# The value projection of an encoder layer by tokens: 128 weight columns moving in place of 384 tokens

## The chip, the cores and the metric

The kernel runs on one core of one Trainium2 chip. The metric is the device time of one execution in microseconds (us), the median of several runs. Before the change it is 1993.51 us, the median of 3 runs (1993.31 to 1993.57).

## What is computed

The kernel does one inference step of a hybrid encoder layer, for 1024 prompt tokens and 128 sample tokens that share the weights. The part that matters here is the projection in front of the forgetting attention, and what becomes of its third piece, the values:

```python
def _in_proj(x, g, w_in, b_f):
    z = _rmsnorm(x, g) @ w_in
    q, k, v, f, u, qm, gates = jnp.split(z, _split_points(), axis=-1)
...
    s = jnp.einsum('bqhd,bkhd->bhqk', q.astype(jnp.float32), k.astype(jnp.float32)) * scale
    s = s + jnp.transpose(cq, (0, 2, 1))[:, :, :, None] - jnp.transpose(ck, (0, 2, 1))[:, None, :]
    s = jnp.where(kpos[None, :] <= qpos[:, None], s, -jnp.inf)
    p = jax.nn.softmax(s, axis=-1)
    o = jnp.einsum('bhqk,bkhd->bqhd', p, v.astype(jnp.float32))
```

The model width is 1024, the values are 512 wide (8 heads of 64). The keys and the values are also outputs, tokens by channels.

## The kernel before

**Tiles.** The normalised activations lie in SBUF with channels on the 128 partitions: `act`, 8 tiles of 128 channels by 1152 tokens (1024 and 128). Each fp32 matrix is kept as two fp32r parts, high and low, and a product is three matmuls (`COMBOS`): high by high, high by low, low by high. A column block of weights is 8 tiles of 128 by 128 (`w_raw`, split by ScalarE and VectorE into `w_hi` and `w_lo`, two sets in turn).

**The plan.** `plan` is a list of steps, written in an order that all engines follow. A step of kind "q", "k", "v", "gate" and so on is one column block of weights by all 1152 tokens. It fills three PSUM banks, one for each 384 tokens. TensorE (`product`, L1230) takes the 128 by 128 weight tile as the stationary operand and 384 tokens of `act` as the moving one, 8 channel tiles by 3 combinations by 3 blocks, so 72 matmuls. The result has channels on the partitions and tokens along them. Each step is cut in `halves`, and work of another kind (attention, sampling, pooling) is put in between them by the table `beside`: before part x of a step, each engine does what is listed for (kind, i, j, x). A bank is used again three blocks later, when it has been emptied (`emptied`).

**A pair of heads.** For each of four pairs of heads (`for p in range(BT)`), the plan has q, k, v, then "kturn" and "vturn", then gate and branch products in which the pair's attention runs (`fox`, 19 pieces). The values leave their bank by a VectorE copy into `vf` (L2078), channels by tokens. In "kturn" and "vturn" TensorE turns keys (`kf`, L1262) and values (`vf`, L1257), three blocks of three 128 by 128 transposes each, in three banks. The turned keys are copied into one of five buffers `tok` by ScalarE (L1598), the turned values by VectorE (L2084). Out of `tok`, the sync engine stores them in DRAM (L766 and L768), and for the values ScalarE makes the high part of `fox_v` (L1635) and VectorE the low part (`values_lo`, L2044). The attention's first scores (L984) stand right behind, in part 0 of the first gate step; VectorE reads them (L1829), ScalarE takes the exponent (L1390). The value product of the attention (L997) takes `fox_v` as one operand.

**What orders them.** `tok_use` numbers the uses of the `tok` buffers, `tok_full` counts them in that order, and `tok_stored` tells when one has been stored. Before, the keys' three come first, then the values' three. `load_negc` loads the attention's bias for pair 0 in part 3 of the first "v" step.

Of the kernel before, what the change touches and what calls it, by code (L numbers as in the profile page):

```python
# [12 lines left out]
P = 128  # L13
# [19 lines left out]
def encoder_program(nc, x_prompt, x_sample, mem_prompt, cache_fox_k, cache_fox_v, cache_fox_logf, cache_pool,  # L33
# [95 lines left out]
    for p in range(BT):  # L129
        add("q", p, src=win[:, :, p * P:(p + 1) * P], hi=3)  # L130
        add("k", p, src=win[:, :, FW + p * P:FW + (p + 1) * P], hi=3)
        add("v", p, src=win[:, :, 2 * FW + p * P:2 * FW + (p + 1) * P])
        add("kturn", p, halves=3)
        add("vturn", p, halves=3, hi=3)
        merge_tile(0, 2 * p)
        merge_tile(0, 2 * p + 1)
    for h in range(MH):
# [65 lines left out]
    with ExitStack() as ctx:  # L203
# [84 lines left out]
        fk = tensor("fox_k", [P, 2, SEQ], R2_AT + 16384, F32R)  # L288
        fv = tensor("fox_v", [P, QT, 4, FD], R2_AT + 24576, F32R)
        kf = tensor("fox_kf", [P, T], R_AT + 8192)  # L290
        vf = tensor("fox_vf", [P, T], R2_AT + 32768)
        fot = tensor("fox_ot", [P, 2 * P], R3_AT + 13824)


# [105 lines left out]


        def tok_use(kind, i, j):
            return {"memturn": i, "kturn": 2 * MH + 6 * i + j, "vturn": 2 * MH + 6 * i + 3 + j,
                    "qm": 2 * MH + 6 * BT + 3 * i + j}[kind]

        def tok_buf(n):
# [12 lines left out]
        def tok_free(eng, kind, i, j, n):  # L419
            k = tok_buf(n)  # L420
            if tok_sent[n]:
                eng.wait_ge(tok_stored[k], tok_sent[n])
            if kind == "kturn" and j == 0 and i:
                for m in range(2):
                    eng.wait_ge(prod_stored[m], 16 * 3 * i)

# [119 lines left out]
        def _(sp):  # L546
# [180 lines left out]
            for s in plan[FIRST:]:  # L727
                for x in range(s.halves):
                    if x == 0 and s.c >= 2:
                        load_weights(sp, s.c + 2)  # L730
                    if s.kind == "qm" and s.i == 0 and x == 4:
                        refill(0)
                    if s.kind == "gate" and s.i == 2 and s.j == 0 and x == 0:
                        refill(1)
                    if s.kind == "q" and s.i and x == 0:
                        load_negc(s.i)
                    if s.kind == "v" and s.i == 0 and x == 3:
                        load_negc(0)
                    if s.kind == "out" and x == 0 and s.i + 1 < KT:
                        load_xtok(s.i + 1)  # L740
                    if s.kind == "br" and s.i == 2 and s.j == KT - 2 and x == 0:
                        load_xtok(0)
                    if s.kind == "gate" and s.i and x >= 3 and (s.i, s.j) != (2, 1):
                        load_prev(s.i, s.j, x - 3)
                    if s.kind == "br" and (s.i, s.j) == (2, 0):
                        load_prev(2, 1, x)
                    for what in beside.get((s.kind, s.i, s.j, x), ()):
                        beside_sp(*what)
                    if s.kind == "memturn" and s.i % 2 == 0:
                        emptied(sp, at["memkv", s.i, 0].b)  # L750
                        sp.dma_start(mem_kt[:, s.i // 2, :], kst[0][:]).then_inc(kst_stored, 16)
                    if s.kind in ("memturn", "kturn", "vturn") or s.kind == "qm" and x % 2:
                        j = x // 2 if s.kind == "qm" else x
                        n = tok_use(s.kind, s.i, j)
                        buf, stored = (tok_q if s.kind == "qm" else tok)[tok_buf(n)], tok_stored[tok_buf(n)]
                        sp.wait_ge(tok_full, n + 1)
                        cs = slice(s.i * P, (s.i + 1) * P)
                        if s.kind == "memturn":
                            cs = slice(s.i // 2 * P, (s.i // 2 + 1) * P)
                            sp.dma_start((mv_out if s.i % 2 else mk_out)[:, :, cs], buf[:, 0:MT, :]).then_inc(stored, 16)  # L760
                        elif s.kind == "qm":
                            sp.dma_start(mem_q[:, s.i, cols(j)], buf[:].rearrange("p t c -> p (t c)")).then_inc(stored, 16)
                        else:
                            big, rest = (kp_out, ks_out) if s.kind == "kturn" else (vp_out, vs_out)
                            tiles = min(3, QT - 3 * j)
                            sp.dma_start(big[:, 3 * j:3 * j + tiles, cs], buf[:, 0:tiles, :]).then_inc(stored, 16)  # L766
                            if j == 2:
                                sp.dma_start(rest[:, cs], buf[:, 2, :]).then_inc(stored, 16)  # L768
                    if s.kind == "br" and s.i < 2:
                        i = 3 * s.j + x  # L770
                        if s.i == 0:
                            emptied(sp, s.b + x)
                        else:
                            sp.wait_ge(mg["added"], i + 1)
                        src = (prod1 if s.i else prod0)[i % 2]
                        sp.dma_start(merged[s.i, s.j, :, cols(x)], src[:]).then_inc(prod_stored[i % 2], 16)
                if s.kind == "k" and s.i == 0:
                    sp.wait_ge(po["tail"], BT)
                    sp.dma_start(new_pool_p.rearrange("l a j c -> (l a j) c"),
                                 p_tail[P - HIST:P, 0, :]).then_inc(po["stored"], 16)  # L780
                    for i in range(NB):
                        sp.dma_start(new_pool_s.rearrange("l b j c -> (l b) j c")[i],
                                     p_tail[(i + 1) * NQ - HIST:(i + 1) * NQ, 1, :]).then_inc(po["stored"], 16)
                if s.kind == "last" and s.i == 0 and s.j == 0:
                    finished(sp, s.b - 1)
                    sp.dma_start(g_y[:], g_final.partition_broadcast(P)).then_inc(g_in["fin"], 16)
# [110 lines left out]
        def _(pe):  # L897
# [348 lines left out]
            def turned(s, x):  # L1246
                b = s.b + x
                emptied(pe, b - 3)
                dst = bank(b)
                if s.kind == "memturn":  # L1250
                    emptied(pe, at["memkv", s.i, 0].b)
                    for t in range(MT):
                        last = nc.tensor.transpose(dst[:, t * P:(t + 1) * P], kst[s.i % 2][:, t * P:(t + 1) * P], ident[:])
                elif s.kind == "vturn":
                    emptied(pe, at["v", s.i, 0].b + x)
                    for t in range(3):
                        last = nc.tensor.transpose(dst[:, t * P:(t + 1) * P], vf[:, (3 * x + t) * P:(3 * x + t + 1) * P],  # L1257
                                                   ident[:])
                else:
                    emptied(pe, at["k", s.i, 0].b + x)  # L1260
                    for t in range(3):
                        last = nc.tensor.transpose(dst[:, t * P:(t + 1) * P], kf[:, (3 * x + t) * P:(3 * x + t + 1) * P],  # L1262
                                                   ident[:])
                last.then_inc(blk_over, 1)

            for s in plan[FIRST:]:
                for x in range(s.halves):
# [2 lines left out]
                    j = x * s.blocks // s.halves  # L1270
                    if s.kind == "memkv":
                        product(s, x, ME, width=NMEM)
                    elif s.kind in ("memturn", "kturn", "vturn"):
                        turned(s, x)
                    elif s.kind == "br":
                        if s.j == 0 and s.i == 0:
                            pe.wait_ge(po["mix_lo"], 3 * BT)
# [27 lines left out]
        def _(act):  # L1305
# [251 lines left out]
            def leave(s, j):  # L1557
# [20 lines left out]
                if s.kind == "br":  # L1578
# [2 lines left out]
                        act.wait_ge(mg["added"], 3 * KT + i + 1)  # L1581
                        nc.scalar.activation(M[0][:, s.j, cols(j)], prod1[i % 2][:], ACT.Copy, scale=0.5).then_inc(mg["hi"], 1)
                    return
                if s.kind in ("v", "down", "last"):
                    return
                finished(act, b)
                if s.kind == "memkv":
# [5 lines left out]
                elif s.kind in ("memturn", "kturn"):  # L1593
                    n = tok_use(s.kind, s.i, j)
                    tok_free(act, s.kind, s.i, j, n)
                    w = MT if s.kind == "memturn" else 3
                    act.wait_ge(tok_full, n)
                    nc.scalar.activation(tok[tok_buf(n)][:, 0:w, :], src[:, 0:w * P].rearrange("p (t c) -> p t c", c=P),  # L1598
# [17 lines left out]
                elif s.kind in ("q", "k"):  # L1616
# [11 lines left out]
                            act.wait_ge(po["tail"], BT)  # L1628
                        last = nc.scalar.activation(rest[0][:, s.i, :], src[:, LAST:TB], ACT.Copy, scale=scale)
                    last.then_inc(ev_hi, 1)  # L1630
                elif s.kind == "vturn":
                    w = min(3, QT - 3 * j)
                    n = tok_use(s.kind, s.i, j)
                    act.wait_ge(tok_full, n + 1)
# [45 lines left out]
        def _(dve):  # L1680
# [369 lines left out]
            def leave(s, j):  # L2050
# [20 lines left out]
                elif s.kind == "v":  # L2071
                    finished(dve, b)
                    if j == 0 and s.i == 0:
                        dve.wait_ge(kst_stored, 16 * MH)
                        finished(dve, at["memturn", 2 * MH - 1, 0].b)
                    elif j == 0:
                        dve.wait_ge(at_s["t_over"], 16 * s.i)
                    nc.vector.tensor_copy(vf[:, cols(j)], src).then_inc(free, 1)  # L2078
                elif s.kind == "vturn":
                    n = tok_use(s.kind, s.i, j)  # L2080
                    finished(dve, b)
                    tok_free(dve, s.kind, s.i, j, n)
                    dve.wait_ge(tok_full, n)
                    nc.vector.tensor_copy(tok[tok_buf(n)][:].rearrange("p t c -> p (t c)"), src).then_inc(tok_full, 1)  # L2084
# [101 lines left out]
```

## Time and profile before

| | |
|---|---|
| median of 3 runs | 1993.51 us (1993.31 to 1993.57) |
| the profiled execution | 1993.0 us, its span from first to last instruction 1991.3 us |
| TensorE matmul busy, share of the span | 98% |
| TensorE weight load busy | 96% |
| VectorE, ScalarE, GpSimd busy | 50%, 32%, 10% |
| TensorE's share of the chain that ended last | 86% |
| mean granted clock of TensorE | 0.997 |

All rows come from one profiled execution. Times in the trace are from the span's start. PE is TensorE's matmul, PEld its weight load, which has rows of its own; DVE is VectorE, ACT ScalarE, SPq the sync engine's issues. The end of a matmul in the trace is modelled, and its start is put down when it was handed to the array; where the array still loads its weights the row becomes longer by that.

### The profile page before, as it was taken

How to read it: one execution, taken by the hardware profiler on the slowest of the kernel's cores; microseconds unless marked ns; L12 is line 12 of the kernel's file. 1: busy time of each engine (PE TensorE's matmuls, PEld its weight loads, DVE VectorE, ACT ScalarE, POOL GpSimd, SP SyncE). 2: the span in 40 equal slices, each digit the busy share in tenths (PEclk: the TensorE clock that was granted, in tenths of full speed). 3: DMA queues.
4: the chain of work that ended last, by engine and by line, in shares of the span. 5: the costliest groups of instructions: out<-in, count | busy, mean ns of one | idle time of the engine just before them, and what ended most of it. 6: DMA issues, size and time to landing. Idle time of an engine off the chain costs nothing.

```text
span 1991.3 us, 28760 instructions
## 1 busy us (share of the span) xinstructions
PE 1950.5 (98%) x11667; PEld 1918.1 (96%) x11667; DVE 987.4 (50%) x1886; ACT 630.6 (32%) x1198; POOL 195.3 (10%) x280
## 2 busy tenths in 40 slices
PE   7999999999999999999999999999999999999998
PEld 7999999999989999999999999999999999999998
DVE  6675545454556465554333455444444444444434
ACT  6444434353545444442223332111111111111112
POOL 0003324251511122000000000000000000000000
PEclk9999999999999999999999999999999999999999
DMA  6451312213166533443233211111101020202202
GB/s 183 117 130 49 90 46 65 79 38 106 34 232 193 188 112 103 147 156 106 83 93 96 71 43 38 33 53 32 53 29 58 27 59 27 59 27 59 70 22 96
DMA packets 208664, 164.24 MB, mean 82 GB/s; under 512 B 15374, under 2 KB 186382, under 8 KB 208533
## 3 DMA queue, kind: packets, MB, share of 16 engines
q1 hardware_dynamic: 208533, 162.41, 26.9%
q8 instruction: 93, 1.52, 0.3%
q14 instruction: 38, 0.31, 0.1%
HBM read 132.86 MB, written 29.51 MB: 82 GB/s over the span
## 4 chain that ended last, share of the span: by engine, by line
PE 86%; DVE 5%; issue 3%; ACT 3%; POOL 2%; DMA 1%; SPq 0%; DVEq 0%; POOLq 0%; ACTq 0%
PE ps L1240 72%; PE ps L1224 3%; PE ps L1076 2%; PE ps L1064 2%; PE ps L997 1%; PE ps L1007 1%; PE ps L1031 1%; POOL fox_p L861 1%; PE ps L912 1%; PE ps L1146 1%; PE ps L984 1%; DVE xs L1693 0%; ACT w_hi L443 0%; ACT fox_pt_hi L1397 0%; PE ps L1133 0%
## 5 line engine op out<-in xcount | busy, mean ns | idle before, releaser
L1240 PE MATMUL ps<-act_hi,w_hi 128*128 128x384 f32 x1800 | 612.5, 340 | 2.0 <-DVE fox_q_lo L2063 0.9
L1240 PE MATMUL ps<-act_hi,w_lo 128*128 128x384 f32 x1800 | 603.6, 335 | 0.0
L1240 PE MATMUL ps<-act_lo,w_hi 128*128 128x384 f32 x1800 | 603.2, 335 | 0.0
L1240 PEld LDWEIGHTS ps<-act_hi,w_hi 128*128 128x128 f32 x1800 | 338.8, 188 | 3.7 <-issue 3.0
L1240 PEld LDWEIGHTS ps<-act_lo,w_hi 128*128 128x128 f32 x1800 | 339.0, 188 | 0.7
L1240 PEld LDWEIGHTS ps<-act_hi,w_lo 128*128 128x128 f32 x1800 | 338.6, 188 | 0.0
L443 ACT ACTIVATE w_hi<-w_raw 128x512 fp32r<-128x512 f32 (+1 forms) x172 | 147.0, 855 | 303.6 <-PE ps L1240 300.8
L461 DVE TENSOR_TENSOR w_lo<-w_raw,w_hi 128x512 fp32r<-128x512 f32 (+1 forms) x172 | 168.1, 977 | 132.5 <-ACT w_hi L443 132.5
L1240 PE MATMUL ps<-ff_hi,w_hi 128*128 128x384 f32 x672 | 227.1, 338 | 0.0
L1240 PE MATMUL ps<-ff_lo,w_hi 128*128 128x384 f32 x672 | 227.1, 338 | 0.0
L1240 PE MATMUL ps<-ff_hi,w_lo 128*128 128x384 f32 x672 | 227.1, 338 | 0.0
L2145 DVE TENSOR_TENSOR h<-ps,h 128x384 f32<-128x384 f32 x192 | 107.0, 557 | 222.2 <-PE ps L1240 198.7
L1576 ACT ACTIVATE ff_hi<-ff_r 128x384 fp32r<-128x384 f32 x96 | 50.4, 525 | 325.7 <-DVE ff_r L2134 325.7
L2134 DVE SCALAR_TENSOR_TENSOR ff_r<-ps,rstd 128x384 f32<-128x384 f32 x96 | 53.5, 557 | 185.1 <-PE ps L1240 185.1
L1240 PEld LDWEIGHTS ps<-ff_hi,w_lo 128*128 128x128 f32 x672 | 126.3, 188 | 0.0
L1240 PEld LDWEIGHTS ps<-ff_hi,w_hi 128*128 128x128 f32 x672 | 126.3, 188 | 0.0
L1240 PEld LDWEIGHTS ps<-ff_lo,w_hi 128*128 128x128 f32 x672 | 126.3, 188 | 0.0
L861 POOL TENSOR_SCALAR fox_p<-fox_p,small 128x128 f32<-128x128 f32 (+7 forms) x64 | 110.5, 1726 | 94.0 <-DVE small L1808 92.2
L1240 PE MATMUL ps<-branch_hi,w_hi 128*128 128x384 f32 x288 | 99.8, 347 | 0.0
L1240 PE MATMUL ps<-branch_hi,w_lo 128*128 128x384 f32 x288 | 96.7, 336 | 0.0
L1240 PE MATMUL ps<-branch_lo,w_hi 128*128 128x384 f32 x288 | 96.4, 335 | 0.0
L1813 DVE TENSOR_TENSOR fox_pt_lo<-ps,fox_pt_hi 128x128 fp32r<-128x128 f32 (+7 forms) x64 | 48.4, 757 | 71.6 <-ACT fox_pt_hi L1397 71.6
(308 smaller groups left out, 2821.4 us busy)
## 6 DMA issues: line engine op xcount, KB each, us to landing
w_raw<-in_w_in_dram SPq DMA_DIRECT2D x44, 512.0 KB, 4.3
w_raw<-in_w_up_dram SPq DMA_DIRECT2D x32, 512.0 KB, 4.1
w_raw<-in_w_down_dram SPq DMA_DIRECT2D x56, 256.0 KB, 2.7
merged<-prod SPq DMA_DIRECT2D x48, 192.0 KB, 1.9
prev<-merged SPq DMA_DIRECT2D x48, 192.0 KB, 4.3
foxs_kraw<-in_cache_fox_k_dram SPq DMA_DIRECT2D x8, 1024.0 KB, 5.6
foxs_vraw<-in_cache_fox_v_dram SPq DMA_DIRECT2D x8, 1024.0 KB, 5.8
out_dram<-fin_y SPq DMA_DIRECT2D x9, 512.0 KB, 2.6
```

The costliest lines, as they stand in the source:

```text
L443: nc.scalar.activation(W[c % 2][0][:, 0:kt, :], w_raw[c % 2][:, 0:kt, :], ACT.Copy).then_inc(w_hi, 1)
L461: nc.vector.tensor_tensor(W[c % 2][1][:, 0:kt, :], w_raw[c % 2][:, 0:kt, :], W[c % 2][0][:, 0:kt, :].bitcast(F32), ALU.subtract).then_inc( ...
L861: nc.gpsimd.tensor_scalar(p, p, col(RC, u), None, ALU.mult).then_inc(at_s["p_ready"], 1)
L912: last = nc.tensor.matmul(bank(s.b)[:, 0:TB], W[k][a][:, t, :], A[z][:, t, cols(s.j)], start=(t == 0 and n == 0), stop=(t == KT - 1 and n ...
L1064: last = nc.tensor.matmul(ps[:, 2 + z, 0:w], stat, b["kt"][y][:, j, z * w:(z + 1) * w], start=first, stop=end)
L1076: last = nc.tensor.matmul(ps[:, 4, :], b["pt"][x][:, t, :], b["v"][y][:, t, :], start=(n == 0 and t == 0), stop=end)
L1224: last = nc.tensor.matmul(bank(s.b)[:, 0:TB], LW[a][:, t, s.j * P:(s.j + 1) * P], AC[(NCH - 1) % 2][z][:, t, cols(s.i)], start=(t == 0 and ...
L1240: last = nc.tensor.matmul(bank(b)[:, 0:width], W[k][a][:, t, :], moving[z][:, t, j * width:(j + 1) * width], start=(t == 0 and n == 0), st ...
L1576: nc.scalar.activation(AC[s.i % 2][0][:, s.j, cols(j)], ff_r[i % 2][:], ACT.Square).then_inc(ff["hi"], 1)
L1813: nc.vector.tensor_tensor(dst[1][:, 0:blocks, cs], turned_tiles()[:, 0:blocks, :], dst[0][:, 0:blocks, cs].bitcast(F32), ALU.subtract).the ...
L2134: nc.vector.scalar_tensor_tensor(out=ff_r[i % 2][:], in0=src, scalar=0.0, in1=rstd[:, cols(j)], op0=ALU.max, op1=ALU.mult).then_inc(free, 1)
L2145: nc.vector.tensor_tensor(h, src, h, ALU.add).then_inc(free, 1)
```

## The change

The "v" step's matmuls exchange their operands: 128 tokens of `act` are the stationary operand, and the 128 columns of a weight tile move. The product then has tokens on the partitions and needs no turning. "vturn" is gone; the "v" step has 9 parts, one for each 128 tokens, and three of them fill a bank. VectorE copies a bank of values straight into `tok`, and the rest of the way (store, high part, low part) is as before. The values' `tok` uses are numbered ahead of the keys'.

```diff
-        add("v", p, src=win[:, :, 2 * FW + p * P:2 * FW + (p + 1) * P])
+        add("v", p, src=win[:, :, 2 * FW + p * P:2 * FW + (p + 1) * P], hi=3, halves=9)
         add("kturn", p, halves=3)
-        add("vturn", p, halves=3, hi=3)
...
-            return {"memturn": i, "kturn": 2 * MH + 6 * i + j, "vturn": 2 * MH + 6 * i + 3 + j,
+            return {"memturn": i, "v": 2 * MH + 6 * i + j, "kturn": 2 * MH + 6 * i + 3 + j,
...
-            if kind == "kturn" and j == 0 and i:
+            if kind == "v" and j == 0 and i:
...
-                    if s.kind in ("memturn", "kturn", "vturn") or s.kind == "qm" and x % 2:
-                        j = x // 2 if s.kind == "qm" else x
+                    if s.kind in ("memturn", "kturn") or s.kind == "qm" and x % 2 or s.kind == "v" and x % 3 == 2:
+                        j = x // 2 if s.kind == "qm" else x // 3 if s.kind == "v" else x
...
-                elif s.kind == "vturn":
-                    emptied(pe, at["v", s.i, 0].b + x)
-                    for t in range(3):
-                        last = nc.tensor.transpose(dst[:, t * P:(t + 1) * P], vf[:, (3 * x + t) * P:(3 * x + t + 1) * P],
-                                                   ident[:])
...
+            def values_product(s, x):
+                j, t = divmod(x, 3)
+                if x == 0:
+                    pe.wait_ge(w_lo, s.c + 1)
+                if t == 0:
+                    emptied(pe, s.b + j - 3)
+                for y in range(KT):
+                    for n, (a, z) in enumerate(COMBOS):
+                        last = nc.tensor.matmul(bank(s.b + j)[:, t * P:(t + 1) * P], A[z][:, y, x * P:(x + 1) * P],
+                                                W[s.c % 2][a][:, y, :], start=(y == 0 and n == 0),
+                                                stop=(y == KT - 1 and n == 2))
+                if t == 2:
+                    last.then_inc(blk_over, 1)
...
+                    if s.kind == "kturn" and j == 2:
+                        act.wait_ge(at_s["v_lo"], 3 * s.i + 1)
...
-                elif s.kind == "vturn":
+                elif s.kind == "v":
                     w = min(3, QT - 3 * j)
                     n = tok_use(s.kind, s.i, j)
                     act.wait_ge(tok_full, n + 1)
...
-                    elif j == 0:
-                        dve.wait_ge(at_s["t_over"], 16 * s.i)
-                    nc.vector.tensor_copy(vf[:, cols(j)], src).then_inc(free, 1)
-                elif s.kind == "vturn":
                     n = tok_use(s.kind, s.i, j)
-                    finished(dve, b)
                     tok_free(dve, s.kind, s.i, j, n)
```

## Rows read from the trace of the kernel before

**Rows 1.** The page: busy time by engine, and the chain by engine.

```profile
PE 1950.5 (98%) x11667; PEld 1918.1 (96%) x11667; DVE 987.4 (50%) x1886; ACT 630.6 (32%) x1198; POOL 195.3 (10%) x280
...
PE 86%; DVE 5%; issue 3%; ACT 3%; POOL 2%; DMA 1%; SPq 0%; DVEq 0%; POOLq 0%; ACTq 0%
```

**Rows 2.** The chain in order of time, at the end of a v product.

```profile
159.09 2.08 PE ps L1240 x12
```

**Rows 3.** The tile fox_vf: min/median/max ns, first and last start.

```profile
L1257 PE MATMUL ps<-ident,fox_vf x36: 272/273/329, 167.4 to 489.2; 128*128 128x128 f32 x36
L2078 DVE COPY fox_vf<-ps x12: 557/558/558, 156.0 to 486.6; 128x384 f32<-128x384 f32 x12
```

**Rows 4.** Timeline, matmuls from 181.2 us: start, duration, instruction.

```profile
181.26 0.22 PE L984 MATMUL ps<-fox_k,fox_q_hi 128*128 128x128 f32 x1
181.32 0.27 PE L984 MATMUL ps<-fox_k,fox_q_lo 128*128 128x128 f32 x1
...
181.72 0.22 PE L997 MATMUL ps<-fox_pt_hi,fox_v 128*128 128x128 f32 x1
181.78 0.28 PE L997 MATMUL ps<-fox_pt_lo,fox_v 128*128 128x128 f32 x1
```

**Rows 5.** Timeline, weight loads of the same stretch.

```profile
181.27 0.19 PEld L984 LDWEIGHTS ps<-fox_k,fox_q_lo 128*128 128x128 f32 x1
181.37 0.19 PEld L997 LDWEIGHTS ps<-fox_pt_hi,fox_v 128*128 128x128 f32 x1
181.49 0.19 PEld L997 LDWEIGHTS ps<-fox_pt_lo,fox_v 128*128 128x128 f32 x1
181.61 0.19 PEld L997 LDWEIGHTS ps<-fox_pt_hi,fox_v 128*128 128x128 f32 x1
181.72 0.19 PEld L997 LDWEIGHTS ps<-fox_pt_lo,fox_v 128*128 128x128 f32 x1
```

**Rows 6.** Timeline, TensorE between the v product and the gate product.

```profile
166.05 0.34 PE L1240 MATMUL ps<-act_hi,w_lo 128*128 128x384 f32 x1
166.23 1.36 PE L1262 MATMUL ps<-ident,fox_kf 128*128 128x128 f32 x9
167.43 1.83 PE L1257 MATMUL ps<-ident,fox_vf 128*128 128x128 f32 x9
...
169.51 0.41 PE L1240 MATMUL ps<-act_hi,w_hi 128*128 128x384 f32 x1
```

**Rows 7.** Timeline, ScalarE and VectorE in and behind that gap.

```profile
166.43 0.56 DVE L2078 COPY fox_vf<-ps 128x384 f32<-128x384 f32 x1 [0.85 <-PE ps L1240]
166.76 0.49 ACT L1598 ACTIVATE tok<-ps 128x384 f32<-128x384 f32 x1 [1.83 <-PE ps L1262]
167.44 0.49 ACT L1598 ACTIVATE tok<-ps 128x384 f32<-128x384 f32 x1 [0.19 <-ACT tok L1598]
...
171.37 0.42 ACT L1635 ACTIVATE fox_v<-tok 128x256 fp32r<-128x256 f32 x1 [0.65 <-DVE tok L2084]
171.42 0.89 DVE L2044 TENSOR_TENSOR fox_v<-tok,fox_v 128x384 fp32r<-128x384 f32 x2
171.80 1.28 ACT L1390 ACT_TABLE_LOAD   x1
```

**Rows 8.** Timeline, the first scores of the attention behind the gap.

```profile
172.24 0.28 DVE L1829 CUSTOM_DVE_ANT_0 fox_p<-ps,fox_negc 128x128 f32<-128x128 f32 x1
172.59 0.39 PE L984 MATMUL ps<-fox_k,fox_q_hi 128*128 128x256 f32 x1 [0.74 <-DVE small L1829]
172.67 0.29 POOL L851 COPY fox_negc<-negc_kept 128x128 f32<-128x128 f32 x1 [23.97 <-DVE small L1829]
...
175.32 0.44 PE L984 MATMUL ps<-fox_k,fox_q_hi 128*128 128x384 f32 x1
```

**Rows 9.** Stretches: length, PE, PEld, DVE, ACT, POOL busy (count), PEclk, DMA.

```profile
166.20:169.50 3.30, 2.99 (x22) 2.13 (x20) 1.12 (x2) 1.57 (x4) 0.00 (x0) 1.00 0.33 97
...
560.80:564.00 3.20, 3.20 (x14) 3.20 (x13) 2.92 (x7) 1.09 (x2) 0.00 (x0) 0.55 1.05 391
```

**Rows 10.** Timeline, matmuls inside the stretch of the lower clock.

```profile
562.16 0.53 PE L1240 MATMUL ps<-act_lo,w_hi 128*128 128x384 f32 x1
562.48 0.53 PE L1240 MATMUL ps<-act_hi,w_lo 128*128 128x384 f32 x1
```

More of the change, by code:

```diff
@@ L290, in encoder_program @@
         kf = tensor("fox_kf", [P, T], R_AT + 8192)
-        vf = tensor("fox_vf", [P, T], R2_AT + 32768)
         fot = tensor("fox_ot", [P, 2 * P], R3_AT + 13824)
@@ L1272, in _ @@
                         product(s, x, ME, width=NMEM)
-                    elif s.kind in ("memturn", "kturn", "vturn"):
+                    elif s.kind in ("memturn", "kturn"):
                         turned(s, x)
+                    elif s.kind == "v":
+                        values_product(s, x)
                     elif s.kind == "br":
@@ L1583, in leave @@
                     return
-                if s.kind in ("v", "down", "last"):
+                if s.kind in ("down", "last"):
                     return
@@ L1630, in leave @@
                     last.then_inc(ev_hi, 1)
-                elif s.kind == "vturn":
+                elif s.kind == "v":
                     w = min(3, QT - 3 * j)
```

## The prediction

> **What bounds the kernel now.** I read the page first. TensorE is the bound: matmuls lie over 98% of the span, weight loads over 96%, and 86% of the chain that ended last is TensorE's; VectorE has 50% and ScalarE 32% [rows 1]. So whatever TensorE gains or loses in the "v" steps reaches the end nearly in full, and work taken from the other engines counts only where TensorE waits for it. Next I read the chain in order of time at the end of a "v" step, for the price of the old product: twelve matmuls with 384 moving columns take 2.08 us, 0.1733 us each [rows 2]. Then I went to the tile that goes, for what its turning costs [rows 3], and to the timeline for the nearest thing to the new product, fp32r matmuls with only 128 moving columns; they exist in the attention's scores and in its value product [rows 4, 5]. Last I read the gap between the value product and the gate product, and the stalls behind it [rows 6, 7, 8].
>
> **The old product.** Four pairs, 72 matmuls each: 72 x 0.1733 = 12.48 us a pair.
>
> **The new product.** 9 token tiles x 8 channel tiles x 3 combinations = 216 matmuls a pair, each with its own load of 128 weight columns. It moves the same number of columns in all, 72 x 384 = 216 x 128. It needs three times as many weight loads. The question is what spaces such matmuls: their columns or their loads. The start times of the matmuls say 0.06 us (181.26 to 181.32, 181.72 to 181.78) [rows 4]. But that start is not the array's. Behind a load that is not yet done the row begins early and grows: of the last two matmuls the first has 0.22 us and the second 0.28. Their ends, 181.94 and 182.06, are 0.12 apart. The loads tell the same: five of them follow each other at 0.10, 0.12, 0.12 and 0.11 us, 0.45 over four, so 0.1125 each [rows 5], although two of the four matmuls between them move 128 columns alone. In the old product a load has 0.1733 us to hide in and costs nothing; over 128 columns it sticks out. I take 0.1125 us: 216 x 0.1125 = 24.3 us. Extra: 24.3 - 12.48 = 11.8 us a pair, 47.3 us for four. Bounds: the shortest and the longest spacing of those loads, 0.10 and 0.12, give 21.6 and 25.9 us, so 36.5 and 53.8 us for four pairs. This step decides the forecast. The granted clock stays at 1.00 through the gap with its transposes [rows 9], so I let the new stream run at the full clock too.
>
> The Trainium skill has a rule that speaks against this change ("TensorE: Matmul & The Clock Gate", section "LDWEIGHTS (loading the stationary operand)"): a weight load takes its column count over 1.2, in ns, so 107 ns for 128 columns. By that the product would take 216 x 0.107 = 23.1 us, an estimate from the page, 1.2 us under mine; the rows of the loads agree with it within 0.01 us.
>
> **What is taken out.** The 9 transposes of values a pair (36 in all) [rows 3]. Nine of keys and nine of values lie between the last value matmul's slot, which ends at 166.05 + 0.17 = 166.22, and the gate product at 169.51 [rows 6]. Of its first row's 0.41 us some 0.07 is the wait for its load (the usual row has 0.34), so the gap is 3.36 us. The transposes within a block follow each other at 0.11 us (a block of nine takes 1.36 with its stop and its tail), so 9 x 0.11 = 1.0 us is work; the rest are stops for the copies.
>
> The new gap, with zero where the value product ends: VectorE's copy of the last value bank starts 0.21 us later (166.43) and takes 0.56, so 0.77. ScalarE's copy into `fox_v`, about 0.1 later, takes 0.42: 1.3. Then comes its copy of the first keys' bank, 0.49: 1.8; the bank is free for the gate product about 0.15 later: 1.95 us [rows 7]. TensorE meanwhile turns the keys (third block behind the bank that is empty at 0.8, done by 1.2) and does the first scores, so it waits some 0.5 us. Gap 1.95 in place of 3.36: 1.4 us saved.
>
> **The stalls behind it.** Part 1 of the gate step begins with the second scores, which wait until VectorE has read the first. VectorE is held up by the turned values, low parts to 172.31, so it reads at 172.24 and TensorE starts at 172.59, with about 1.0 us lost: the gate's 12 matmuls of part 0, at 2.08 us from 169.58, would have ended at 171.66 [rows 7, 8]. After the change values 0 and 1 are copied and split under the value product; only the third remains. VectorE is free at about 1.8 us and TensorE asks at 4.0, so the 1.0 us goes. In part 2 there is another stall: 172.94, when the gate goes on behind the second scores, plus 2.08 is 175.02, and the third scores start at 175.32, some 0.3 to 0.4 late [rows 8]. What is late is the chain of ScalarE: table load, exponent, weight split, then VectorE's part. It starts 5.6 us behind the product now (171.80 - 166.22) and 1.3 + 3 x 0.68 = 3.3 us behind it then (the three copies of keys stand 0.68 apart), 2.3 earlier; TensorE also comes 2.4 us earlier. So this stall stays, perhaps 0.1 longer. Sum: 1.4 + 1.0 - 0.1 = 2.3 us a pair, 9.2 for four. Bounds: the transposes alone, 9 x 0.11 x 4 = 4.0, and all stalls gone, 4 x (1.4 + 1.0 + 0.4) = 11.2.
>
> **What costs nothing.** The 12 VectorE copies of 0.56 us [rows 3] lie under TensorE's work; so do the new copies of blocks 0 and 1, with some 8 us of product (24.3 / 3) behind each, which also covers ScalarE's and VectorE's parts of 0.5 and 0.6 us. The splits of the gate's weights, at the start of "v", get more cover than before. On the sync engine's queue the stores of values now stand ahead of `load_negc(0)`, of pair 0 alone, which waits for the first block, some 8 us and a copy into the step. GpSimd was done with its masks 23.97 us before 172.67, at 148.7 [rows 8], and they are needed at the first scores, which come 12 us later than before, so there are some 15 us left for a load and a few masks of 0.29 us. The waits on `tok_stored` meet stores that were issued 8 us or more ahead; the wait of ScalarE in "kturn" for the first low part is long over. The wait for all stores ahead of the gate's first evacuation comes 4 us behind the last issue, as before.
>
> **Sum.** 1993.0 us (the profiled execution, 1991.3 in the span) + 47.3 - 9.2 = 2031.1 us; the median of the runs is 0.5 above that execution, so about 2031.5.
>
> **The rivals.** (a) The loads are hidden after all and the stream runs at the 0.06 us of the start times [rows 4]: 216 x 0.06 = 13.0, +0.5 a pair, +1.9 - 9.2 = -7.3, so 1986 us, faster. Against it stand the ends and the loads' own spacing. It is the case on the other side; it decides from (12.48 + 2.3) / 216 = 0.068 us a matmul downwards. (b) Half of the load is hidden in a long stream, the mean of 0.06 and 0.1125: 0.086 us, 18.6 us a pair, +24.6 - 9.2 = +15.4, so 2009 us. For it: no stretch of before has more than two such matmuls in a row. The Trainium skill states for a stream with a load at each matmul and 128 columns about 81 ns (same page, "Back-to-back issue gap"), by which the time would be 2005 us, an estimate; no row here shows that spacing. (c) Load and stream come one after the other, 0.1125 + 0.06 = 0.1725: 37.3 us a pair, +99.1 - 9.2 = +90, so 2083 us. Against it: in the old product a load would then never be hidden, yet it fits in 0.1733 with 384 columns [rows 2]. (d) The granted clock falls in the new stream. After the wait at 560 it stood at 0.55, the lower level of 1.2 GHz for most of the stretch, and matmuls came 0.32 us apart in place of 0.17 [rows 9, 10], 1.85 times. If the loads slow down likewise: 24.3 x 0.85 x 4 = 83 more, so 2114 us. Against it: it fell only behind a long wait, and there is none in the stream. (e) The load has its price, and the gap gives back only the transposes: 2037 us, inside the range.
>
> **Chances.** My forecast with (e) and the bounds of the load: 0.82. (a) 0.05, (b) 0.05, (c) 0.04, (d) 0.02, anything else 0.02. A difference of 0.2% (4 us) is about what can be told from none. Faster 0.05, same 0.01, slower 0.94. The range: low 1993.5 + 36.5 - 9.2 = 2020.8, high 1993.5 + 53.8 - 4.0 = 2043.3; together 0.82, as wanted, so 2021 to 2043.
>
> **What the profile after will show.** Right: weight loads with `act` stationary and w moving about 0.11 us apart, some 24 us for each v product, matmul rows over 0.2 us in spite of a spacing half as long; TensorE without stops inside a "v" step; a gap of about 2 us up to the gate; no stall at part 1 of the gate and a short one at part 2. Wrong: loads 0.06 to 0.09 apart, a granted clock under 1 inside "v", a wait for a bank at a block's start, or GpSimd late at the first scores of pair 0.

## The result

The changed kernel takes 2031.05 us (median of 4 runs, 2029.74 to 2032.25); the kernel before, measured beside it, 1993.41 (1991.94 to 1993.57). The ratio is 1.0192, with a 95% interval of 1.018 to 1.0204: slower by 37.6 us. The forecast was 2031.5, with 2021 to 2043 as its range. The profiled execution has a span of 2029.1 us, 37.8 more than before.

The page of the changed kernel, its counterpart to [rows 1]:

```profile
PE 1989.2 (98%) x12207; PEld 1959.8 (97%) x12207; DVE 982.6 (48%) x1874; ACT 630.9 (31%) x1198; POOL 196.1 (10%) x280
...
PE 87%; DVE 4%; issue 4%; ACT 2%; POOL 1%; DMA 1%; SPq 0%; ACTq 0%; DVEq 0%; POOLq 0%
```

There are 540 matmuls more: 4 x (216 - 72) = 576, less 36 transposes. In the rows that follow L1268 is the new product, L1238 the ordinary one. The bound is the same engine, and its time has grown.

The chain in order of time in the v step of the second pair, which answers to [rows 2], and the stretch of that step, with the granted clock behind the busy times:

```profile
269.89 23.56 PE ps L1268 x211
```

```profile
269.20:293.20 24.00, 24.00 (x218) 24.00 (x216) 4.50 (x8) 3.03 (x6) 0.00 (x0) 1.00 0.06 17
```

23.56 / 211 = 0.1117 us a matmul, at a clock of 1.00 and without a stop: 216 x 0.1117 = 24.1 us, against 12.48. The weight loads at the end of the first pair's step, which answer to [rows 5], stand 0.11 apart as well:

```profile
176.55 0.19 PEld L1268 LDWEIGHTS ps<-w_lo,act_hi 128*128 128x128 f32 x1
176.67 0.19 PEld L1268 LDWEIGHTS ps<-w_hi,act_hi 128*128 128x128 f32 x1
176.78 0.19 PEld L1268 LDWEIGHTS ps<-w_hi,act_lo 128*128 128x128 f32 x1
176.89 0.19 PEld L1268 LDWEIGHTS ps<-w_lo,act_hi 128*128 128x128 f32 x1
```

TensorE's timeline from the last value matmul on (L1255 the keys' transposes, L982 the scores), answering to [rows 6, 8]:

```profile
176.95 0.28 PE L1268 MATMUL ps<-w_lo,act_hi 128*128 128x128 f32 x1
177.06 1.42 PE L1255 MATMUL ps<-ident,fox_kf 128*128 128x128 f32 x9
178.24 0.31 PE L982 MATMUL ps<-fox_k,fox_q_hi 128*128 128x128 f32 x1
...
178.91 0.41 PE L1238 MATMUL ps<-act_hi,w_hi 128*128 128x384 f32 x1 [0.25 <-ACTq L1613]
...
181.08 0.28 PE L982 MATMUL ps<-fox_k,fox_q_hi 128*128 128x256 f32 x1
...
183.76 0.44 PE L982 MATMUL ps<-fox_k,fox_q_hi 128*128 128x384 f32 x1 [0.19 <-DVE small L1841]
```

The gap goes from 177.06 to 178.98 (178.91 and 0.07 of the long row), 1.92 us in place of 3.36. What ends it is ScalarE's copy of the first keys' bank (L1613 is its release of the bank). The second scores come 181.08 - 178.98 = 2.10 us into the gate step, which is the step's own pace: the stall of 1.0 us is gone. The third come at 183.76; the gate goes on at 181.32, and twelve matmuls from there end at 183.40, so a stall of 0.4 us remains. This second stall is in the first pair only: in the other three, before and after, the third scores follow the gate's matmuls at once. The ScalarE and VectorE rows behind the product, counterparts to [rows 7]:

```profile
177.92 0.42 ACT L1647 ACTIVATE fox_v<-tok 128x256 fp32r<-128x256 f32 x1 [7.52 <-PE ps L1255]
178.24 0.48 ACT L1610 ACTIVATE tok<-ps 128x384 f32<-128x384 f32 x1
178.91 0.49 ACT L1610 ACTIVATE tok<-ps 128x384 f32<-128x384 f32 x1 [0.19 <-ACT tok L1610]
```

```profile
177.26 0.56 DVE L2091 COPY tok<-ps 128x384 f32<-128x384 f32 x1 [6.78 <-PE ps L1268]
177.97 0.89 DVE L2056 TENSOR_TENSOR fox_v<-tok,fox_v 128x384 fp32r<-128x384 f32 x2
```

Before their last piece VectorE was idle for 6.78 us and ScalarE for 7.52: the first two blocks lie wholly under the product.

### The profile page after: what moved, and what is told of

Same layout as the page of the kernel before. It is cut to its first block, busy times and chain, and to the rows that moved or that the text cites. A ratio compares the mean times of both kernels' runs of the same rounds, so it can differ in the third digit from the quotient of the medians.

```text
span 2029.1 us, 29817 instructions
## 1 busy us (share of the span) xinstructions
PE 1989.2 (98%) x12207; PEld 1959.8 (97%) x12207; DVE 982.6 (48%) x1874; ACT 630.9 (31%) x1198; POOL 196.1 (10%) x280
## 4 chain that ended last, share of the span: by engine, by line
PE 87%; DVE 4%; issue 4%; ACT 2%; POOL 1%; DMA 1%; SPq 0%; ACTq 0%; DVEq 0%; POOLq 0%
PE ps L1238 68%; PE ps L1268 5%; PE ps L1222 2%; PE ps L1074 2%; PE ps L1062 2%; PE ps L995 1%; PE ps L910 1%; PE ps L1005 1%; PE ps L1029 1%; POOL fox_p L859 1%; PE ps L1144 1%; PE ps L982 1%; ACT fox_pt_hi L1407 0%; DVE prod L2110 0%; ACT w_hi L441 0%
## 5 line engine op out<-in xcount | busy, mean ns | idle before, releaser
L1238 PE MATMUL ps<-act_hi,w_hi 128*128 128x384 f32 x1704 | 579.7, 340 | 2.3 <-ACTq L1613 1.0
L1238 PE MATMUL ps<-act_hi,w_lo 128*128 128x384 f32 x1704 | 570.7, 335 | 0.0
L1238 PE MATMUL ps<-act_lo,w_hi 128*128 128x384 f32 x1704 | 570.3, 335 | 0.0
L1238 PEld LDWEIGHTS ps<-act_hi,w_hi 128*128 128x128 f32 x1704 | 320.5, 188 | 4.1 <-issue 3.3
L1238 PEld LDWEIGHTS ps<-act_lo,w_hi 128*128 128x128 f32 x1704 | 320.6, 188 | 0.7
L1238 PEld LDWEIGHTS ps<-act_hi,w_lo 128*128 128x128 f32 x1704 | 320.1, 188 | 0.0
L1238 PE MATMUL ps<-ff_hi,w_hi 128*128 128x384 f32 x672 | 227.0, 338 | 0.0
L1238 PE MATMUL ps<-ff_lo,w_hi 128*128 128x384 f32 x672 | 227.0, 338 | 0.0
L1238 PE MATMUL ps<-ff_hi,w_lo 128*128 128x384 f32 x672 | 227.0, 338 | 0.0
L1238 PEld LDWEIGHTS ps<-ff_hi,w_lo 128*128 128x128 f32 x672 | 126.2, 188 | 0.0
L1238 PEld LDWEIGHTS ps<-ff_hi,w_hi 128*128 128x128 f32 x672 | 126.2, 188 | 0.0
L1238 PEld LDWEIGHTS ps<-ff_lo,w_hi 128*128 128x128 f32 x672 | 126.2, 188 | 0.0
L1238 PE MATMUL ps<-branch_hi,w_hi 128*128 128x384 f32 x288 | 99.7, 346 | 0.0
L1238 PE MATMUL ps<-branch_hi,w_lo 128*128 128x384 f32 x288 | 96.7, 336 | 0.0
L1238 PE MATMUL ps<-branch_lo,w_hi 128*128 128x384 f32 x288 | 96.4, 335 | 0.0
```

The source lines that it names most:

```text
L1238: last = nc.tensor.matmul(bank(b)[:, 0:width], W[k][a][:, t, :], moving[z][:, t, j * width:(j + 1) * width], start=(t == 0 and n == 0), st ...
```

## The experiments

All are measured against the kernel before, in runs on the same chip (1991.5 to 1992.6 us there).

**The turning alone (`turn_gone`).** In the changed kernel the product is the old one again, in its usual parts; the main line of the edit:

```diff
-                        values_product(s, x)
+                        product(s, x, A)
```

> The turning taken out alone: the value product stays as it was (72 matmuls of 384 moving columns a pair), its banks go straight into tok, so the value outputs and the attention's values hold channels by tokens; nothing else is left out. Theory (the gap closes and the stall goes): the changed kernel's trace has a gap of 1.92 us in place of 3.36 and no stall at part 1 of the gate step (1.0 us), so 4 x 2.44 = 9.8 us less than before: 1983.6 us. Rival (only the transposes' own work comes back, 36 x 0.11 = 4.0 us): 1989.4 us.

Measured: 1983.03 us against 1992.28, ratio 0.9954 (0.9942 to 0.9967), 9.3 us less. Its timeline behind the product has the changed kernel's gap, from 166.05 to 167.96, and second scores at 170.05, without a stall:

```profile
165.88 0.34 PE L1238 MATMUL ps<-act_hi,w_lo 128*128 128x384 f32 x1
166.06 1.42 PE L1255 MATMUL ps<-ident,fox_kf 128*128 128x128 f32 x9
...
167.89 0.41 PE L1238 MATMUL ps<-act_hi,w_hi 128*128 128x384 f32 x1 [0.25 <-ACTq L1613]
```

The first theory holds. Of the 9.3 us only some 4.0 are the transposes' own time (36 x 0.11, an estimate from their spacing); the rest were stops. With the keys' turning and all copies out of `tok` left as they are, this is what turning the values for nothing would give back.

**The product alone (`product_only`).** In the kernel before, "v" runs `values_product` in 9 parts, and "vturn" and all else stays.

> The product by tokens alone: 216 matmuls a pair with 128 moving columns, and the values are turned all the same, so they reach the attention and the outputs turned the wrong way. Theory (each matmul costs 0.111 us, nothing hides it): 216 x 0.111 = 24.0 in place of 12.48 us a pair, 46.1 us in all: 2039.5 us. Rival (the longer step also gives or takes waits elsewhere, in the sampling stage for one, where the changed kernel lost a further 1 to 2 us): off from that by over 1.5 us.

Measured: 2041.02 us (2038.96 to 2044.25) against 1992.28, ratio 1.0247 (1.0233 to 1.0261). That is 48.7 more, with a spread of 5 us between its runs; 46.1 was expected, and the interval of the ratio (46.4 to 52.0 us) lies just above it. The rival asked for over 1.5 us of difference, and against the kernel before beside it there are 2.6, so it holds. Where the difference arises the trace tells. When the sampling stage begins (its first transpose of cached keys, 606.23 us against 560.07) the kernel is 46.2 us behind, the theory's number, and only at the first matmul with `ff_hi`, the feed-forward's (1317.39 against 1270.12), is it 47.3. The price of the product is thus as forecast, and the rest is picked up in other stages; why there is not shown. The sum of the two halves is -9.25 + 48.74 = 39.5 us, against 37.6 for the whole. The halves add up within the spread of the runs, and whether the 2 us between them are more than that is not settled.

**The values turned first (`values_first`).** The kernel before with two steps exchanged, and the numbers of `tok_use` with them:

```diff
-        add("kturn", p, halves=3)
         add("vturn", p, halves=3, hi=3)
+        add("kturn", p, halves=3)
```

> The kernel before with the values turned ahead of the keys, nothing left out. Theory (the stall of 1.0 us at part 1 of the gate step is VectorE's being held up by the turned values): it goes, and the gap grows by some 0.3 us a pair because ScalarE's first copy of keys now waits for three VectorE copies: 4 x 0.7 = 2.8 us less, 1990.6 us. Rival (VectorE's order does not matter, the stall only moves into the gap): 1993.4 us.

Measured: 1992.02 us against 1992.28, ratio 0.9999 (0.999 to 1.0007). The rival holds: no gain. TensorE's timeline in the gap, here from 166.25:

```profile
166.25 1.42 PE L1257 MATMUL ps<-ident,fox_vf 128*128 128x128 f32 x9
167.59 0.55 PE L1262 MATMUL ps<-ident,fox_kf 128*128 128x128 f32 x3
168.38 0.55 PE L1262 MATMUL ps<-ident,fox_kf 128*128 128x128 f32 x3 [0.25 <-DVEq L2088]
169.56 0.55 PE L1262 MATMUL ps<-ident,fox_kf 128*128 128x128 f32 x3 [0.62 <-DVEq L2088]
...
170.52 0.41 PE L1240 MATMUL ps<-act_hi,w_hi 128*128 128x384 f32 x1 [0.25 <-ACTq L1603]
...
172.68 0.28 PE L984 MATMUL ps<-fox_k,fox_q_hi 128*128 128x256 f32 x1
```

The second scores are in time (172.68 - 170.59 = 2.09), but the gap is 4.34 us in place of 3.36. The last block of keys now waits for a bank that VectorE empties last, and ScalarE copies its first keys only then. So the stall at part 1 did come of VectorE's being late, as read from [rows 7, 8], but order alone only moves the loss into the gap.

**High and low weights side by side (`wide_moving`).** The changed kernel with one matmul of 256 moving columns for two of 128:

```diff
+                            last = nc.tensor.matmul(bank(s.b + x)[:, 0:2 * P], A[0][:, y, x * P:(x + 1) * P],
+                                                    W2[s.c % 2][:, :, y, :], start=(y == 0), stop=(y == KT - 1))
```

> The changed kernel with high and low weights side by side as 256 moving columns: the high activations are loaded once for both, 144 loads a pair in place of 216, same columns; VectorE adds the two halves of a bank. Nothing is left out. Theory (a matmul costs its weight load, 0.111 us, where its columns take less): 72 x (0.120 + 0.111) = 16.6 in place of 24.0 us a pair, 29.5 us less than the changed kernel: 2001.5 us. Rival (128 moving fp32r columns cost 0.111 us by themselves, whatever the loads): 256 columns cost 0.222 and nothing changes: 2031 us.

Measured: 1999.19 us (1998.29 to 2000.59) against 1992.28, ratio 1.0034 (1.0021 to 1.0047), so some 31 us less than the changed kernel, and still 6.9 us more than before. Two loads, one for 256 columns and one for 128, take 0.23 us together:

```profile
270.14 0.19 PEld L1273 LDWEIGHTS ps<-w_both,act_hi 128*128 128x128 f32 x1
270.25 0.19 PEld L1270 LDWEIGHTS ps<-w_both,act_lo 128*128 128x128 f32 x1
270.37 0.19 PEld L1273 LDWEIGHTS ps<-w_both,act_hi 128*128 128x128 f32 x1
```

The same columns with a third fewer loads cost 16.6 us a pair (72 x 0.23) in place of 24.1, so the columns are not the cost. This run has a third fewer matmuls too, and so it can't tell the price of a load from a fixed price of a matmul; `narrow_standing`, below, does.

**Fewer moving columns, or fewer standing ones (`narrow_moving`, `narrow_standing`, `narrow_96`).** In the changed kernel the matmuls with a low part are made smaller, but for the last of each tile (135 of 216 a pair), once in the weights that move (64, and later 96), once in the tokens that stand (64):

```diff
+                        m = P if n == 0 or n == 2 and y == KT - 1 else P // 2
+                        last = nc.tensor.matmul(bank(s.b + j)[:, t * P:t * P + m], A[z][:, y, x * P:(x + 1) * P],
+                                                W[s.c % 2][a][:, y, 0:m], start=(y == 0 and n == 0),
```

> The changed kernel with only 64 weight columns moving in 135 of the 216 matmuls a pair (those with a low part, but for each tile's last), so the low parts are left out for half of the value columns. The loads stay at 128 columns. Theory (the load sets the spacing): no change, 0.111 us each, 2031 us. Rival (the moving columns set it): these take half, 0.056 us, 135 x 0.055 x 4 = 30 us less: 2001 us.

> The changed kernel with only 64 tokens standing in the same 135 matmuls a pair, so the low parts are left out for half of the tokens; all 128 weight columns move. Theory (the load sets the spacing): a load of 64 columns takes half, and the stream of 128 columns (0.06 us) sets it then: 135 x 0.05 x 4 = 27 us less, 2004 us. Rival (the moving columns set it): no change, 2031 us.

Measured: `narrow_standing` 2004.2 us (3 runs, 2003.19 to 2004.38) against 1991.54, ratio 1.0062 (1.0039 to 1.0084), on the theory's 2004. That is 12.7 us more than before, so 25 us less than the changed kernel's 37.6. Its loads of 64 columns stand 0.06 apart, those of 128 0.11, at a clock of 1.00, though there are as many loads, matmuls and moving columns as in the changed kernel. So it is the standing columns, and not the number of matmuls, that are paid for:

```profile
168.53 0.19 PEld L1269 LDWEIGHTS ps<-w_hi,act_hi 128*128 128x128 f32 x1
168.64 0.14 PEld L1269 LDWEIGHTS ps<-w_hi,act_lo 128*64 128x64 f32 x1
168.70 0.13 PEld L1269 LDWEIGHTS ps<-w_lo,act_hi 128*64 128x64 f32 x1
168.76 0.19 PEld L1269 LDWEIGHTS ps<-w_hi,act_hi 128*128 128x128 f32 x1
```

`narrow_moving` 2094.49 us (2 runs, 2094.39 and 2094.58), ratio 1.0516 (1.0485 to 1.0546): half the columns in most of the matmuls, and 63 us slower than the changed kernel. Neither theory nor rival had that. The stretches (length, busy times, and behind them the granted clock), and loads from before and after the fall:

```profile
165.00:170.00 5.00, 5.00 (x45) 5.00 (x45) 1.23 (x3) 0.69 (x2) 1.47 (x5) 1.00 0.11 43
170.00:175.00 5.00, 5.00 (x34) 5.00 (x33) 0.50 (x1) 0.41 (x1) 0.00 (x0) 0.70 0.12 39
175.00:180.00 5.00, 5.00 (x25) 5.00 (x25) 0.00 (x0) 0.00 (x0) 0.00 (x0) 0.50 0.00 0
```

```profile
168.42 0.19 PEld L1269 LDWEIGHTS ps<-w_hi,act_lo 128*128 128x128 f32 x1
168.53 0.19 PEld L1269 LDWEIGHTS ps<-w_lo,act_hi 128*128 128x128 f32 x1
...
178.42 0.33 PEld L1269 LDWEIGHTS ps<-w_hi,act_hi 128*128 128x128 f32 x1
178.63 0.33 PEld L1269 LDWEIGHTS ps<-w_hi,act_lo 128*128 128x128 f32 x1
```

At the full clock (2.4 GHz) the theory holds to the digit: 0.11 us a load, though most matmuls move half as much. Then the clock falls to 0.50 (1.2 GHz) in the middle of the stream, with loads and matmuls back to back, and a load takes 0.21.

> As the changed kernel with 64 columns moving in 135 of the 216 matmuls a pair, but with 96 moving; the low parts are left out for a quarter of the value columns. With 64 the loads came 0.112 us apart until the granted clock fell to the lower level inside the stream, and 0.213 behind that. Theory (the fall comes of how little the array moves between the loads, and 96 is enough): the clock stays at 1.00 in the v steps, loads 0.112 us apart, 2030 us, the same as with 128 columns. Rival (it falls here too, and the changed kernel with 128 columns is close to it): 0.2 us a matmul behind the fall, 2050 to 2090 us.

Measured: 2033.02 us (2 runs) against 1992.57, ratio 1.0204 (1.0186 to 1.0222). Clock and spacing in its v steps are those of the changed kernel:

```profile
160.00:176.00 16.00, 16.00 (x141) 16.00 (x140) 3.49 (x6) 2.68 (x5) 1.47 (x5) 1.00 0.29 92
```

So between 96 and 128 moving columns there is no difference in spacing either, and no fall of the clock; of the runs here only the one with 64 has it.

**Keys turned under the value product (`keys_beside`).** `turn_gone` says that stops are worth over 5 us, and `values_first` that order alone does not remove them. So the old product stays, the keys are turned in its parts 2 to 4 in two banks of the attention that are free then, and VectorE's low parts move behind its second scores:

```diff
-        add("kturn", p, halves=3)
+            put(("v", p, 0, 2 + j), "kturn", p, j)
+        put(("gate", 0, 2 * p, 1), "vlo", p)
```

> The kernel before (384 tokens moving, values turned), nothing left out. The keys are turned in parts 2 to 4 of the v step, in two banks that the attention does not use yet, and only the values are turned in the gap; VectorE makes the values' low parts in part 1 of the gate step, behind its reading of the second scores. Theory (the time between value product and gate is set by copies that follow each other, and part 1 stalls because VectorE is busy with the values): the gap shrinks from 3.36 to about 1.65 us, 1.0 of which goes into the v step, and the stall of 1.0 us goes: 4 x 1.7 = 7 us less, 1985.5 us. Rival (as with the values turned first, the stall only moves, here to part 2, behind VectorE's later low parts): within 1 us of 1992.3.

Measured: 1987.3 us (median of 9 runs) against 1992.57 (14 runs), ratio 0.9972 (0.9962 to 0.9982): 5.3 to 5.6 us less, where 7 were expected. Eight of the nine runs lie between 1985.2 and 1988.42; the ninth took 4960.19 us, is not in the ratio, and no trace of it shows why. It is the only version here that leaves nothing out and beats both kernels. Two things were changed at once, the place of the keys' turning and that of the low parts, and what each gives by itself was not measured. The gap is 1.50 us (167.20 to 168.70), the second scores are in time:

```profile
167.03 0.34 PE L1272 MATMUL ps<-act_hi,w_lo 128*128 128x384 f32 x1
167.20 1.42 PE L1289 MATMUL ps<-ident,fox_vf 128*128 128x128 f32 x9
...
168.64 0.40 PE L1272 MATMUL ps<-act_hi,w_hi 128*128 128x384 f32 x1
...
170.79 0.29 PE L1000 MATMUL ps<-fox_k,fox_q_hi 128*128 128x256 f32 x1
...
174.08 0.44 PE L1000 MATMUL ps<-fox_k,fox_q_hi 128*128 128x384 f32 x1 [0.79 <-DVE small L1873]
```

In the first pair the third scores stall by 1.0 us (the gate's matmuls end at 173.12), more than the 0.3 of before, and that costs the pair 0.7 us: from its first scores to the next pair's, 0.8 us are gained in the first pair, 1.5 and 1.6 in the second and third. The place is the one that the rival named, but not its reason: VectorE's low parts start at 173.94, when it has read the second scores. The other pairs have no such stall. What only the first pair has is a table load on ScalarE:

```profile
170.56 1.28 ACT L1422 ACT_TABLE_LOAD   x1
```

```profile
180.24 1.28 ACT L1400 ACT_TABLE_LOAD   x1
```

The first row is of `keys_beside`, the second of the changed kernel. Exponent, weight split and VectorE's part follow it, and the third scores start 3.52 us behind it in both (174.08, 183.76), as in the kernel before (171.80 to 175.32) [rows 7, 8]. ScalarE starts the load when its last copy of keys or values is done. A shorter gap brings TensorE to that point sooner, and there it waits for this chain.

## Why the prediction was right

**The price of the new matmul** (0.1125 us from four load spacings): right in mechanism and size. It measured 0.1117, so 46.6 us in four pairs in place of 47.3. The ground given, that loads and not start times set the pace, is shown: fewer loads for the same columns cost 7.5 us less a pair (`wide_moving`), and fewer standing columns shorten the spacing (`narrow_standing`) where fewer moving ones, at the same clock, do not (`narrow_moving` up to its fall, `narrow_96`). Rivals (a), (b) and (c) are out: in the second pair's step 214 of the 215 spacings between its loads are 0.11 and one, behind its first load, is 0.17, where the last matmul of 384 columns from the step before still runs. The four spacings that the forecast rests on were thin evidence: two of the four matmuls among them moved 256 columns, so they alone could not tell a load's price from a stream's.

By the Trainium skill's rule in "TensorE: Matmul & The Clock Gate", "LDWEIGHTS (loading the stationary operand)", a load of 128 columns takes 107 ns; the trace has 111.7 in a long stream, so it agrees within 5%. The 81 ns that the Trainium skill gives in "Back-to-back issue gap" of the same page for 128 columns does not hold for these fp32r matmuls, which stand 111.7 ns apart (and by the prediction's own terms 81 ns makes 2004 us, not 2005).

**The gap** (3.36 to 1.95): measured 1.92, with the chain of copies that was drawn up.

**The stall at part 1** (1.0 us to nothing): gone in all four pairs; it was 0.9 us in each. **The stall at part 2** (0.1 longer in each pair): wrong in its number of pairs. It went from 0.3 to 0.4 us in the first pair, and the other three never had it, so its term was some 0.1 us for all four and not 0.4. The prediction read one pair and took the others to be like it.

**The sum.** The forecast is 0.45 us off, but that closeness is in part luck. The starts of the same instructions in the two profiled executions show where the difference grew (us from the span's start):

| | before | after | later by |
|---|---|---|---|
| first matmul of the first v step | 151.11 | 150.36 | -0.75 |
| first transpose of keys, first pair | 166.23 | 177.06 | 10.83 |
| the same, fourth pair | 486.42 | 524.74 | 38.32 |
| first transpose of the sampling's cached keys (`foxs_kraw`) | 560.07 | 595.82 | 35.76 |
| first scores of the sampling tokens (`foxs_qpad`) | 568.13 | 606.33 | 38.20 |
| first matmul with `ff_hi` | 1270.12 | 1307.98 | 37.87 |

From the first row to the fourth the change costs 36.5 us: 46.35 for the four longer products (11.58 and three times 11.59; 47.3 forecast), less 9.85 for gaps and stalls (9.2 forecast). By its own terms the forecast was thus 1.6 us too high. What makes up for most of that lies outside them. The changed kernel's execution is 0.75 us ahead when the first v step begins, and it loses 2.4 us between the sampling's first transpose and its first scores:

```profile
560.07 1.09 PE L1031 MATMUL ps<-ident,foxs_kraw 128*128 128x128 f32 x8 [2.25 <-DMA foxs_kraw<-in_cache_fox_k_dram]
...
564.65 1.03 PE L1031 MATMUL ps<-ident,foxs_kraw 128*128 128x128 f32 x8
...
568.13 0.51 PE L1064 MATMUL ps<-foxs_kt_hi,foxs_qpad_hi 128*128 128x264 f32 x2 [0.36 <-DVE foxs_qpad_lo L1896]
```

```profile
595.82 1.09 PE L1029 MATMUL ps<-ident,foxs_kraw 128*128 128x128 f32 x8 [2.18 <-DMA foxs_kraw<-in_cache_fox_k_dram]
...
601.28 1.05 PE L1029 MATMUL ps<-ident,foxs_kraw 128*128 128x128 f32 x4 [2.28 <-DVE foxs_kt_lo L1895]
...
606.33 0.51 PE L1062 MATMUL ps<-foxs_kt_hi,foxs_qpad_hi 128*128 128x264 f32 x2 [0.24 <-DVE foxs_qpad_lo L1908]
```

The first three rows are of before, the others of after. This stretch takes 8.06 us before and 10.51 after, but 7.57 in `product_only`, which has the same long product, and between 7.5 and 10.1 in the other runs. So it can't be put down to the longer product, and its cause is not shown.

**The cover on GpSimd.** Its masks for the first pair are made at 165.0 to 167.0, and VectorE reads the first scores at 178.8, so the later load of the bias costs nothing. The cover is 11.8 us and not 15: the first scores come 9.2 us later than before (178.24 against 169.01), not 12.

```profile
165.05 0.29 POOL L836 COPY negc_kept<-fox_negc 128x128 f32<-128x128 f32 x1 [161.09 <-DMA fox_negc<-negc_prompt]
```

**What was weak: the argument against rival (d).** The prediction said that the clock "fell only behind a long wait, and there is none in the stream". The changed kernel's clock did stay at 1.00, but the reason does not hold: in `narrow_moving` it fell without any wait. Against (d) only the outcome speaks.

**The range.** Its low end takes the gain of 9.2 us and not the prediction's own bound of 11.2, with which it would be 2019. Nothing hangs on it here.

## What to carry to other kernels

A matmul with its own weight load costs the longer of the two: here 0.112 us for the load of 128 fp32r columns, which 384 moving columns (0.173 us) cover and 128 do not. So before operands are exchanged to spare transposes, count the loads: the 36 transposes were 4 us of work, or 9.3 with the stops around them, and 576 more matmuls with a load each cost 46.6. What a turning step costs beyond its work are the copies around it, and over 5 us were had by turning the keys under the old product and making the low parts later (`keys_beside`). And look for a stall that you read in one pair of heads in the others too, before you multiply it by four.

## What was not expected of the hardware

The granted clock fell from 2.4 to 1.2 GHz inside a stream of back-to-back loads and matmuls, with both rows busy throughout, when 135 of 216 matmuls moved only 64 columns; with 96 or 128, and in `narrow_standing`, it stayed at 1.00. Why it falls is not shown. The load slowed with it, from 0.11 to 0.21 us for 128 columns. The fall came in each of the four pairs. The smaller product took 42.9 and 42.6 us in the last two in place of 24.1, and 58 of the 63 us lie in the four products.
